# Block sums and seven products: pairs of column units in the two middle groups of a squared-ReLU MLP

## The reference, cut to what matters

```python
v = rms_norm(h, g_mlp)                                   # 256 x 2048
h = h + jnp.square(jax.nn.relu(v @ w_mlp_up)) @ w_mlp_down   # 2048 -> 8192 -> 2048
```

## Time and profile before

| what | value |
|---|---|
| median of three runs | 1570.45 us |
| profiled execution, its own time | 1570.37 us |
| its span, first to last instruction | 1568.6 us |
| TensorE (PE) busy | 1560.0 us, 99% |
| VectorE (DVE) busy | 1073.4 us, 68% |
| ScalarE (ACT) busy | 925.5 us, 59% |
| GpSimd (POOL) busy | 147.8 us, 9% |
| share of PE in the chain that ended last | 99% |

### The profile page before, as it was taken

How to read it: one execution, slowest core, us unless ns; L and a number is a source line. 1 busy time by engine, 2 the same in 40 slices (tenths; PEclk the granted TensorE clock), 3 DMA queues, 4 the chain that set the end, 5 groups by cost and what they waited for, 6 DMA issues and landing times.

```text
span 1568.6 us, 19800 instructions
## 1 busy us (share of the span) xinstructions
PE 1560.0 (99%) x7186; PEld 1287.6 (82%) x7186; DVE 1073.4 (68%) x1287; ACT 925.5 (59%) x1372; POOL 147.8 (9%) x247
## 2 busy tenths in 40 slices
PE   9999999999999999999999999999999999999998
PEld 8888887878878888888888888888888888888887
DVE  6679988768999958986655545565456555656665
ACT  6574466655454555767687544773467535777754
POOL 0222376443000000000000000000000000000000
PEclk9999999999999999999999999999999999999999
DMA  9766566656766668876656666666666666666663
GB/s 324 269 197 194 161 208 221 196 194 188 216 201 211 205 211 298 281 264 207 193 181 203 200 191 188 200 188 201 190 187 199 192 195 188 191 199 194 221 193 130
DMA packets 93764, 324.25 MB, mean 207 GB/s; under 512 B 10864, under 2 KB 14448, under 8 KB 93296
## 3 DMA queue, kind: packets, MB, share of 16 engines
q1 hardware_dynamic: 93536, 322.88, 66.0%
q10 hardware_dynamic: 144, 0.26, 0.1%
HBM read 312.62 MB, written 10.49 MB: 206 GB/s over the span
## 4 chain that ended last, share of the span: by engine, by line
PE 99%; ACT 0%; ACTq 0%; issue 0%; POOL 0%; DVE 0%; POOLq 0%
PE ps L427 32%; PE ps L429 31%; PE ps L428 31%; PE ps L731 0%; PE ps L734 0%; PE ps L988 0%; PE ps L987 0%; PE ps L989 0%; PE ps L737 0%; PE ps L815 0%; PE ps L840 0%; PE ps L891 0%; PE ps L715 0%; PE ps L902 0%; PE ps L802 0%; PE ps L746 0%
## 5 line engine op out<-in xcount | busy, mean ns | idle before, releaser
L410 DVE TENSOR_TENSOR sb<-sb,sb 128x1024 fp32r<-128x1024 f32 x552 | 676.8, 1231 | 407.6 <-ACT sb L403 402.3
L403 ACT ACTIVATE sb<-sb 128x1024 fp32r<-128x1024 f32 x552 | 581.9, 1057 | 522.2 <-PE ps L429 492.1
L427 PE MATMUL ps<-sb,sb 128*128 128x512 f32 (+1 forms) x2176 | 846.6, 389 | 0.0
L428 PE MATMUL ps<-sb,sb 128*128 128x512 f32 (+1 forms) x2176 | 843.8, 388 | 0.0
L429 PE MATMUL ps<-sb,sb 128*128 128x512 f32 (+1 forms) x2176 | 843.7, 388 | 0.0
L427 PEld LDWEIGHTS ps<-sb,sb 128*128 128x128 f32 x2176 | 408.4, 188 | 88.8 <-issue 4.2
L429 PEld LDWEIGHTS ps<-sb,sb 128*128 128x128 f32 x2176 | 408.4, 188 | 84.3
L428 PEld LDWEIGHTS ps<-sb,sb 128*128 128x128 f32 x2176 | 408.5, 188 | 83.1
L473 ACT ACTIVATE ps<-ps 32x256 f32<-32x256 f32 x464 | 162.8, 351 | 29.6 <-DVE ps L462 23.6
L1321 POOL TENSOR_TENSOR sb<-sb,sb 128x1 f32<-128x1 f32 x1 | 0.6, 560 | 1172.5 <-DVE sb L1990 1172.5
L499 POOL COPY sb<-sb 32x256 f32<-32x256 f32 (+1 forms) x112 | 76.0, 679 | 189.0 <-DVE sb L491 184.6
(11 more groups left out here) (238 smaller groups left out, 601.8 us busy)
## 6 DMA issues: line engine op xcount, KB each, us to landing
sb<-in_w_gate SPq DMA_DIRECT2D x128, 512.0 KB, 3.9
sb<-in_w_up SPq DMA_DIRECT2D x128, 512.0 KB, 3.9
sb<-in_w_down SPq DMA_DIRECT2D x128, 512.0 KB, 4.1
sb<-in_w_mix SPq DMA_DIRECT2D x56, 512.0 KB, 4.3
sb<-in_w_branch SPq DMA_DIRECT2D x32, 512.0 KB, 4.7
sb<-in_w_out SPq DMA_DIRECT2D x32, 512.0 KB, 3.8
sb<-in_w_pg SPq DMA_DIRECT2D x32, 512.0 KB, 4.0
gate_mem<-sb SPq DMA_DIRECT2D x16, 512.0 KB, 5.3
```

The costliest lines, as they stand in the source:

```text
L403: act.activation(whi[:, j % RING, :], raw[:, j % RING, :], ACT.Copy).then_inc(hi_done, 1)
L410: eng.tensor_tensor(wlo[:, j % RING, :], raw[:, j % RING, :], whi[:, j % RING, :].bitcast(F32), ALU.subtract).then_inc(lo_done, 1)
L427: pe.matmul(o, xh, w_h, start=first and k == 0, stop=False)
L428: pe.matmul(o, xh, w_l, start=False, stop=False)
```

## The change

In groups 1 and 2 the units are taken by pairs: up units 0 and 1, up 2 and 3, down 0 and 1, down 2 and 3, called here pairs 1 to 4 (p = 0 to 3 in the code). A pair is 16 tiles in which the two units alternate. Tiles 2j and 2j+1 make step j: the same 256 rows for 2 x 512 columns, that is a product of a 2 x 2 grid of token and row blocks with a 2 x 2 grid of weight blocks, 8 block products of 3 matmuls each. In steps 2 and 5 (`SEVEN`, tiles 4, 5 and 10, 11) the 8 become 7 by Winograd's sums: four sums of activation blocks (`token_sums`) and four sums of weight blocks (`t_raw`), which also need a high and a low part. The products that do not go straight into one output are gathered in four temporary banks, which are the PSUM of the pair next door (`temp_bank`), and are added up in slot 12.

Since `side` now holds results, the squared ReLU is turned in SBUF (`pair_lane`). GpSimd moves the 16 blocks of a pair's first unit, ACT those of the second. ACT also squares, and ReLU follows the sum on DVE instead of reading PSUM.

```diff
@@ pe
+                for i in range(2 * TPU):
+                    j, c = divmod(i, 2)
...
+                    if p == PAIRS // 2 and i in (0, TPU, TPU + TPU // 2):
+                        pe.wait_ge(tp_lo, g * NCH + (TP_FF + {0: NCH - 2, TPU: NCH - 1}.get(i, NCH)))
+                    if j in SEVEN:
...
+                        pe.wait_ge(lo_done, u * TPU + (jj + 1))
+                        three(temp_bank(p, 0), half(x_hi_, 0, 0), half(x_lo_, 0, 0), block(whi, s, 0), block(wlo, s, 0),
+                              first, last)
+                        three(main_bank(p, 0, 0), half(x_hi_, 1, 0), half(x_lo_, 1, 0), block(whi, s, 1), block(wlo, s, 1),
+                              False, False).then_inc(tile_used, 1)
+                        pe.wait_ge(lo_done, u * TPU + (jj + 2))
+                        if up:
+                            pe.wait_ge(up_sums_lo, len(SEVEN))
+                        else:
+                            pe.wait_ge(dn_sums_lo, g * len(SEVEN) + (e + 1 - len(SEVEN)))
...
+                        three(temp_bank(p, 1), sh(1), sl(1), t_high[:, 0, :], t_low[:, 0, :], first, last)
@@ pe, around the loop
             mlp_group(0, True, False)
             with pe.Fori(1, NFG - 1) as g:
-                mlp_group(g, False, False)
+                for p in range(PAIRS):
+                    pair_of_units(g, p)
+            pe.wait_ge(temps_free, (NFG - 2) * PAIRS + 1)
             mlp_group(NFG - 1, False, True)
@@ act
+                    if p in (1, 2):
+                        n = 2 * (p - 1)
+                        if i == 0:
+                            relu_square(1, p - 1)
+                        if i in (4, 5, 7):
+                            if i == 4:
+                                act.wait_ge(strips_done, g * NCH + (TP_FF + n + 2))
+                            for m in range(*{4: (0, 5), 5: (5, 10), 7: (10, 16)}[i]):
+                                ins = act.activation(*pair_block(1, m), ACT.Copy)
...
+                        if i in (6, 9):
+                            n += i == 9
+                            act.wait_ge(tp_in, g * NCH + (TP_FF + n + 1))
...
@@ gpsimd
+            for g in range(1, NFG - 1):
+                for q in range(0, NCH, 2):
+                    gp.wait_ge(strips_done, g * NCH + (TP_FF + q + 1))
+                    for i in range(16):
+                        ins = gp.tensor_copy(*pair_block(0, i))
+                    ins.then_inc(tp_in, 1)
@@ vector
+                    if t - 1 in STEP_TILES:
...
+                        v.tensor_tensor(wlo[:, s, C:2 * C], raw[:, s, C:2 * C], whi[:, s, C:2 * C].bitcast(F32), ALU.subtract)\
+                            .then_inc(lo_done, 1)
+                        for b in range(2):
+                            v.wait_ge(comb_hi, g * per + (2 * (len(SEVEN) * (p - PAIRS) + e) + b + 1))
+                            v.tensor_tensor(t_low[:, 2 * b:2 * b + 2, :], t_raw[:, 2 * b:2 * b + 2, :],
+                                            t_high[:, 2 * b:2 * b + 2, :].bitcast(F32), ALU.subtract).then_inc(comb_lo, 1)
...
+                    else:
+                        v.wait_ge(hi_done, u * TPU + (jj + AHEAD + 1))
+                        v.tensor_tensor(wlo[:, s, :], raw[:, s, :], whi[:, s, :].bitcast(F32), ALU.subtract)
...
+                        linked(v.tensor_tensor(t_raw[:, 0:2, :], raw[:, s + 1, :].rearrange("p (k n) -> p k n", k=2),
+                                               raw[:, s:s + 2, 0:C], ALU.subtract))
+                        v.sem_inc(comb_raw, 1)
+                        linked(v.tensor_tensor(t_raw[:, 2, :], t_raw[:, 1, :], raw[:, s, 0:C], ALU.add))
+                        linked(v.tensor_tensor(t_raw[:, 3, :], raw[:, s, C:2 * C], t_raw[:, 2, :], ALU.subtract))
+                        v.sem_inc(comb_raw, 1)
+                        v.sem_inc(lo_done, 1)
```

More of the change, by code:

```diff
@@ L120 @@
 S5_C_TILE, S5_B_TILE = 3, 20
+PAIRS = NCH
+SEVEN = (2, 5)
+STEP_TILES = [2 * j for j in SEVEN]
+PAIR_STEPS = 46
 LEAD, BETWEEN = TPU - 2, 2
@@ L298, in hybrid_layer, with sums_at @@
         g_fin = at(rc[0], [D])
+        r = Region(*rc)
+        t_at, s_up_at, s_dn_at = r.off, r.off + size((8, CW)), r.off + size((12, CW))
+        assert s_dn_at + size((4, CW)) <= r.end
+        t_raw, t_low, t_high = at(t_at, [4, CW]), at(t_at, [4, CW], F32R), at(t_at + size((4, CW)), [4, CW], F32R)
+        extra = at(t_at, [2, TT, CW])
+        def sums_at(off):
+            return (at(off, [2, 4, P]), at(off, [2, 4, P], F32R), at(off + size((2, 4, P)), [2, 4, P], F32R))
+        up_raw, up_low, up_high = sums_at(s_up_at)
+        dn_raw, dn_low, dn_high = sums_at(s_dn_at)
+        whole = at(t_at, [TK, S])
+        pair_lane = [scratch[:, 0, :], at(top, [TT * CW])]
         acc = [ctx.enter_context(nc.psum_tensor(f"ps{i}", [P, 2 * CW], F32)) for i in range(2)]
@@ L1228, in mlp_group @@
                             quad_hi(act, g * NCH + (TP_FF + n - 1), side_of(TP_FF + n - 1), f_hi[:, 4 * n - 4:4 * n, :])
+                        if first and n == 6 and j in (2, 4):
+                            act.wait_ge(up_sums, j // 2)
+                            act.activation(up_high[:, j // 2 - 1, :, :], up_raw[:, j // 2 - 1, :, :], ACT.Copy)\
+                                .then_inc(up_sums_hi, 1)
                         if first and n == 0 and t == 4:
@@ L1910, in mlp_group @@
                                     f_hi[:, 4 * n - 4:4 * n, :])
+                        if first and n == 6 and j in (1, 3):
+                            up_token_sums(j // 2)
+                        if first and n == 6 and j in (3, 5):
+                            e = (j - 3) // 2
+                            v.wait_ge(up_sums_hi, e + 1)
+                            v.tensor_tensor(up_low[:, e, :, :], up_raw[:, e, :, :], up_high[:, e, :, :].bitcast(F32),
+                                            ALU.subtract).then_inc(up_sums_lo, 1)
                         if first and n == 0 and t == 4:
@@ L1919, in _, with linked @@
             mlp_group(0, True, False)
+            v.sem_inc(temps_free, 1)
             with v.Fori(1, NFG - 1) as g:
-                mlp_group(g, False, False)
+                count = [0]
+                def linked(ins):
+                    count[0] += 1
+                    ins.then_inc(pair_step, 1)
+                    v.wait_ge(pair_step, g * PAIR_STEPS + (count[0] - PAIR_STEPS))
+                for p in range(PAIRS):
+                    pair_of_units(g, p, linked)
+                assert count[0] == PAIR_STEPS, count[0]
```

193 lines of the change are left out of this document (191 added, 2 removed).

## The result

The changed kernel takes 1583.26 us (median of 4 runs, 1583.14 to 1584.02) against 1570.24 us of the kernel before beside it: ratio 1.0084, 95% interval 1.0066 to 1.0101. It is slower by 13.0 us; 7.8 us were forecast. The profiled execution took 1583.19 us, its span is 12.8 us longer.

The account below looks back on a forecast made before the run. TensorE was taken to bound the kernel, with time to spare on ACT and DVE: -10.9 + 1.5 + 2 x (4.3 + 3.0 + 1.3) = +7.8 us, so 1578.2 us, range 1571 to 1586 us.

Parts of the forecast that it names:

- What bounds, and the saving: TensorE, busy 99% of the span, bounds; 48 matmuls dropped in the two middle groups save 10.9 us.
- The chain second turning, ten moves, rounding: Pair 3 before tile 8: DVE turns the second unit by 17.4, ACT moves and rounds until 24.1 us.
- Term 4: Pair 2, step 5: DVE releases tile 10 late, TensorE waits 1.3 us per group, bounds 0 to 2.
- Term 2: Pair 3, tile 8: 3.6 us of waiting for a low part plus 0.7 us at tile 4, 4.3 us per group.
- One sign: DVE's line 444 should wait for ACT in pairs 1 and 4 and hardly in pair 3.
- Term 1: Entry to pair 1 of group 1: TensorE waits for DVE's last sum of group 0, 1.5 us, once.
- Term 3: Pair 3, step 5: TensorE waits 3.0 us per group behind an 11.0 us DVE list ending with the token sums' low part.
- The clock: Rival: TensorE's clock falls after the new stops, about 2.8 us lost per fall, 1581 to 1589 us; chance 0.14.
- GpSimd as the last: Rival: GpSimd's 16 copies wait for whole DVE instructions and end last, +2 x 7.6, 1593 us; chance 0.06.
- the clock's middle case: Middle of the clock rival's one to four falls (1581 to 1589 us); it set the range's upper end, 1586 us.

Follow-up runs that it names:

- no_steps: The changed kernel without any step of seven products, so 8 products in every step, no weight or token sums, no temporary banks: 1571.0 us, ratio 1.0005.
- turn1_p3_plain: The changed kernel with the second unit's turning in slot 1 for slot 3 on DVE and no steps of seven products in pair 3: 1563.93 us, ratio 0.9959.
- turn1: The changed kernel with the turning of a pair's second unit moved on DVE from slot 3 to slot 1: 1572.4 us, ratio 1.0014.
- keep_warm: The changed kernel with zero matmuls ahead of tile 10 in pair 2, tile 8 in pair 3 and pair 3's token sums wait: 1583.28 us, ratio 1.0082.
- the probe: The kernel before with 14 stops put into TensorE's stream in groups 0 and 3, by waits for GpSimd memsets of 256 to 4096 columns: 1608.0 us.
- plain5_warm: The changed kernel with step 5 of pair 3 by 8 products and zero matmuls ahead of pair 2's tile 10 and pair 3's tile 8: 1578.8 us, ratio 1.0055.

## Why the prediction was right, and where its sizes were off

**What bounds, and the saving.** Right: 48 matmuls fewer, and the saving is paid in full where nothing waits. The spans of no_steps (no matmul saved) and turn1_p3_plain (36 saved) are 7.1 us apart: 36 x 0.227 = 8.2 us less two short stops of 0.5 us.

**The chain second turning, ten moves, rounding.** Right as a mechanism: turn1 moves one instruction pair and both stops vanish. The mis-sized parts are ACT's moves, 0.43 us from start to start where I took 0.36 us from moves within PSUM and had given 0.42 us as the upper end (ten lie on the path to either stop; in pair 2 the other six come behind the split of tile 10), and the signals behind linked instructions (0.33 us for two, 0.2 us taken). Term 4 is what suffers: 2.3 us for 1.3 us, just above the bound of 2. Term 2's stop is 4.2 us for 3.6 us, 4.5 us with the clock up. One sign failed: DVE's line 444 was to wait for ACT hardly in pair 3, and it waits there for 2.16 and 1.99 us in group 1, during ACT's moves. So DVE has a pause in that chain although its list is late at step 5.

**Term 1.** The step "a signal 0.1 us" behind "the sum 1.23 us" failed. The wait was 0.42 us, because the signal doesn't stand behind the sum: DVE started it at 950.56 and TensorE went on at 950.87, before its end. In the table's measure that is 0.6 us for 1.5 us. Only the second tile waits for the sum itself.

```profile
950.56 1.22 DVE L2063 TENSOR_TENSOR sb<-ps,sb 128x1024 f32<-128x1024 f32 x1 [0.41 <-PE ps L463]
...
950.87 0.49 PE L1035 MATMUL ps<-sb,sb 128*128 128x512 f32 x1 [0.42 <-DVEq L2225]
```

**Term 3.** As it stands in the trace it seems wrong (0.2 to 0.4 us for 3.0 us). keep_warm and turn1 show the list as it was worked out (2.9 and 3.0 us in the table's measure); the fallen clock had used that time up beforehand.

**The rivals.** The clock did fall, but the price given to it, 2.8 us for each fall on top of the forecast, was wrong: 9.1 us of slow matmuls changed the time by 0.0 us in the pair changed kernel and keep_warm. The step that failed is the addition: a loss on TensorE was added to waits of TensorE that follow it in the same chain. GpSimd as the last was rightly refused here, and by 0.26 us it is true once the turning is early. The Trainium skill, "TensorE: Matmul & The Clock Gate", section "Why this matters for your kernels", advises against idle gaps between bursts; the probe agrees for its four stops of 2.77 us and more. keep_warm and plain5_warm add that here a fall cost time only where no later wait of TensorE took it up.

**Sum.** With the clock up the waits are 11.7 us per group and 0.6 us at the entry for 8.6 and 1.5 us forecast. The missing 3.1 us per group are 0.9 in term 2, 1.0 in term 4, and about 1.0 in short delays that no term had: 0.1 us behind each stop, tile 9 of pair 2 (0.2) and a second short wait in the first step of pair 3. That 1583 us lies inside the range is partly luck. The bounds of the terms themselves reach -10.9 + 1.5 + 2 x (5.0 + 3.0 + 2.0) = +10.6 us, 1581 us; the range went on to 1586 us for the clock's middle case, and the price in that case is what the runs refute.

## What to carry to other kernels

Fewer products on the bounding engine pay only if the sums that they need don't stand in front of a chain that ends at it; look at what the new instructions push back in an in-order list, not only at the engine's busy share. A stop and the slow matmuls behind it aren't added to a later wait whose last input comes at its own time: work out when that input is ready. Moving one pair of instructions and giving up a quarter of the steps turned a loss of 13.0 us into a gain of 6.5 us.

## What the runs showed of the hardware

- Behind an otherwise full stream, TensorE's clock stayed up behind ten stops of 0.43 to 2.35 us and fell behind four of 2.77 to 3.63 us; in the changed kernel it fell behind 2.10 and 2.12 us and behind 4.06 and 4.07 us, and in turn1 behind one of two equal stops (2.86 and 2.87 us). The loss was 1.3 to 3.0 us.
- A stop delays TensorE by 0.27 us more than the wait that the profile shows (0.68 us for 0.42 at the entry, 2.62 us for 2.35 in the probe): 0.16 us because the wait is counted from the end of the matmul before, 0.1 us in the distance of the first two matmuls behind it (0.34 us for 0.23).
- An ACT copy of 32 x 256 takes 415 ns from SBUF to SBUF and 351 ns within PSUM.
- A signal that followed a DVE instruction without a wait for it had released TensorE 0.3 us after that instruction's start (950.56 to 950.87), 0.9 us before its end.
- Beside GpSimd's copies each DVE instruction with two SBUF inputs took 0.2 us more, and a copy up to 1.4 us in place of 0.39 us (13.7 us for sixteen). The Trainium skill, "SBUF — State Buffer", section "Who interferes with whom", gives the exclusive lock on the shared ports as the reason; the rows agree.
